# One memory map for the attention, index and sparse stages of a two-block transformer kernel, with the first loads of each stage issued in the stage ahead and the index tiles taken from most to fewest keys

## The chip, the cores and the metric

The kernel runs on one core of a Trainium2 chip. The metric is device time in microseconds (us), the median of several executions. Engines are called PE (TensorE), ACT (ScalarE), DVE (VectorE), POOL (GpSimd) and SP (SyncE, which here only issues DMAs).

## What is computed

A sequence of 2048 rows of width 1024 goes through two blocks. This case concerns the first, which joins a latent attention (MLA) and a sparse attention (DSA). Cut to what matters:

```python
h = rms_norm(x, norm_gain)
(c_q, c_kv, k_pe, gate_a, q_b, k_b, v_b, gate_b, q_i, k_i, w_i, m_a, m_b) = split(h @ w_in)
...
o_a = mla_attention(q_a, k_a, v_a) * silu(gate_a)            # 8 heads, causal, 96 wide
rel = relu(einsum('bqhd,bsd->bqhs', q_i, k_i))               # index: 8 heads, 32 wide
score = where(causal, einsum('bqhs,bqh->bqs', rel, w_i), -inf)
_, sel = top_k(score, 256)
o_b = attention over the keys in sel (8 heads, 2 kv heads) * silu(gate_b)
merged = sigmoid(m_a + b0) * (o_a @ w_branch_mla) + sigmoid(m_b + b1) * (o_b @ w_branch_dsa)
x = x + merged @ w_out
```

The second block (a window attention with sinks) follows and is not touched.

## The kernel before

The program is a row of stages, with a barrier of all engines between them (`sem.end_stage`, line 70 is where an engine waits at one): front (projections), MLA attention, index, sparse attention (DSA), merge, banded attention, final. Stages hand over through DRAM tensors (`scratch_...`). Products in high precision are three matmuls, hi and lo parts (`mm3`, lines 93 to 95).

**Front** (`stage_front`) computes, tile by tile of 128 rows, everything that the attentions read, and SP stores it to `scratch_qkT`, `scratch_va` and so on. Its loop counts slots n, twelve per row tile.

**Attention** (`stage_attention`, with a layer `Mla` or `Dsa`) works in 32 units. Of MLA, a unit is a head and a group of 512 rows (odd heads take the groups in reverse); of DSA a tile of 128 rows and one of two kv heads. For each unit PE makes scores, DVE adds the mask and takes the maximum (line 1042), ACT the exponential (1107), PE transposes (1012), ACT and DVE split into hi and lo (1115, 1072), PE multiplies with the values, POOL finishes the output. SP issues the loads of unit n + 4 (`layer.load`) and the stores of unit n - 1, in one queue.

**Index** (`stage_index`) does two things at once. One is the scores and the selection of 256 keys for row tiles 2 to 15 (tiles 0 and 1 have no more than 256 keys): step I is one head's product with up to 1024 keys (line 1409), then ACT's relu (1441) and DVE's weighted sum into `i_score` (1564, 1567); step M sets the bounds of a bisection (DVE 1574 to 1581, after POOL's mask); ten steps H halve it, each ACT's `Sign` with a count (1452) and then POOL's next threshold (1514, 1518); step T (DVE, 1587 to 1630) counts, and takes the rest with MAX8 and MATCH_REPLACE8; in it step R (PE, 1416) brings one number to one partition. POOL then stores the mask of the tile. The other is the gates: 24 chunks of 128 weight columns times 4 groups of 512 rows, that is 96 units of 8 steps G, each three matmuls of 128 x 512 (tile `i_p_g`, three banks), evacuated by ACT (1468, 1470) into two buffers and stored by SP. The weights come through one buffer `i_ws` and are split by ACT (step W, 1460) and DVE (1549).

`index_steps` writes the order of all these by hand: a tile's share of the G steps follows a cost, and its steps I and H are spread over that share. All engines walk the same list:

```python
marks += [((x + 0.5) / len(heads), 1, step) for x, step in enumerate(heads)]
marks += [((i + 0.5) / HALVINGS * 0.95, 0, ("H", before, i)) for i in range(HALVINGS)]
marks.append((AFTER_TOP / share, 2, ("R", after)))
```

So while PE and ACT do the I steps of tile t and the H steps of tile t - 1, DVE first has step T of tile t - 2. `i_relu` has three buffers, `i_p_s` two. Tiles go from 2 to 15, so the selection of the largest tile stands alone at the end. POOL loads the index queries of a tile in the middle of the halvings of the tile two before it (`load(t + 2)` after the sixth halving), four DMAs.

Every stage allocates its memory anew from the same base, so a stage's first loads are issued after the barrier: in MLA 5 DMAs per unit on SP for units 0 to 3, in index the weights, hT (the transposed input, 8 DMAs of 2 MB, for 4 groups) on SP and queries and keys on POOL, in DSA queries, mask, keys hi and lo and values in four groups on SP.

Of the kernel before, what the change touches and what calls it, by code (L numbers as in the profile page):

```python
# [22 lines left out]
P = 128  # L23
# [8 lines left out]
H = 8  # L32
# [107 lines left out]
def stage_front(nc, sem, ident, a, h_dram, qkT, qbT, kbT, qiT, kiT, va, vb, wi, bias):  # L140
# [18 lines left out]
    with ExitStack() as c:  # L159
# [95 lines left out]
        def _(sp):  # L255
# [558 lines left out]
class Attention:  # L814
# [26 lines left out]

    def sync_unit(self, sp, n): ...
# [54 lines left out]
def stage_attention(nc, sem, tag, ident, layer):  # L897
# [13 lines left out]
    with ExitStack() as c:  # L911
        sb = lambda n, s, d=F32: c.enter_context(nc.sbuf_tensor(f"{tag}_{n}", s, d))
        probs = sb("probs", [P, R, 4, layer.width])
# [21 lines left out]
        layer.setup(nc, sem, ident, c, dict(exped=exped, inverted=inverted, multiplied=multiplied, moved=moved,  # L935
# [23 lines left out]
        def _(pe):  # L959
# [37 lines left out]
            for step in steps:  # L997
# [8 lines left out]
                elif step[0] == "B":  # L1006
# [4 lines left out]
                    for s in range(s0, 4):  # L1011
                        last = nc.tensor.transpose(p_t[:, ring(n, place), s * P:(s + 1) * P],  # L1012
                                                   probs[:, n % R, s, j * P:(j + 1) * P], ident[:])
# [17 lines left out]
        def _(dve):  # L1031
            layer.dve_start(dve)
            i = 0
            for step in steps:
                if step[0] == "S":
                    _, n, s, ch, k0, w, last = step
                    if ch == 0:
# [5 lines left out]
                        out=probs[:, n % R, s, k0:k0 + w], in0=p_s[:, i % A, 0:w],  # L1043
# [53 lines left out]
        def _(act):  # L1097
            layer.act_start(act)
            for step in steps:
                if step[0] == "E":  # L1100
                    _, n, s = step
                    act.wait_ge(shifted, n + 1 if layer.batched else n_sub(n, s) + 1)
                    x = probs[:, n % R, s, 0:units[n]["keys"][s]]
# [38 lines left out]
class Mla(Attention):  # L1142

    scale = QK ** -0.5

    def __init__(self, qkT, va, oT, bias_job):
        self.qkT, self.va, self.oT, self.bias_job = qkT, va, oT, bias_job
# [4 lines left out]
                      for _, g in self.of]  # L1152

    def setup(self, nc, sem, ident, ctx, sems):
        sb = lambda n, s, d=F32: ctx.enter_context(nc.sbuf_tensor(f"mla_{n}", s, d))
        self.nc, self.sems = nc, sems
        self.q = [sb(f"q_{n}", [QK, 2, T], F32R) for n in ("hi", "lo")]
        self.k = [sb(f"k_{n}", [QK, 2, T], F32R) for n in ("hi", "lo")]
        self.v = sb("v", [P, 2, NT, P], F32R)
        self.none = sb("none", [P, GT])  # L1160
        self.causal = sb("causal", [P, GT])
        self.first_in, self.in_ = sem("mla_first_in", NG), sem("mla_in", 2)
# [23 lines left out]
    def load(self, sp, n):  # L1186
        h, g = n // NG, n % NG
# [10 lines left out]
        for half in range(2):  # L1198
            sp.dma_start(self.q[half][:, p, at].bitcast(F32), self.qkT[half, h, :, at]).then_inc(done, 16)
            sp.dma_start(self.k[half][:, p, at].bitcast(F32), self.qkT[half, H + h, :, at]).then_inc(done, 16)  # L1200
# [12 lines left out]
    def scores(self, out, n, s, k0, w):  # L1213
        p, t = n // NG % 2, self.of[n][1] * 4 + s
        q = [x[:, p, t * P:(t + 1) * P] for x in self.q]
        k = [x[:, p, k0:k0 + w] for x in self.k]
# [30 lines left out]
AFTER_TOP = 10  # L1247


def index_steps(tiles, chunks):  # L1250
# [5 lines left out]
    total = NG * len(gate_chunks()) * KD  # L1256
    tiles = list(tiles)
    keys = lambda t: P * (t + 1)
    cost = [0] + [8.5e-3 * (keys(t) + keys(t - 1)) + 7 for t in tiles[1:]] + [8.5e-3 * keys(tiles[-1]) + 20]
    steps, given = [("W", 0), ("W", 1)], 0  # L1260

    def give(count):
        nonlocal given
        for _ in range(min(count, total - given)):
            step, k = divmod(given, KD)
            steps.append(("G", step, k))
            given += 1
            if k == KD - 1 and step % NG == 0:
                n = step // NG + 1
                if 2 <= n < len(gate_chunks()):  # L1270
                    steps.append(("W", n))

    passed = 0
    for n, t in enumerate(tiles + [None]):
        before, after = tiles[n - 1] if n else None, tiles[n - 2] if n >= 2 else None
        passed += cost[n]
        share = int((total - AFTER_TOP) * passed / sum(cost) + 0.5) - given
        marks = []
        if t is not None:
            heads = [("I", t, h, k0, width) for h in range(H) for k0, width in chunks(t)]  # L1280
            marks += [((x + 0.5) / len(heads), 1, step) for x, step in enumerate(heads)]
        if before is not None:
            marks += [((i + 0.5) / HALVINGS * 0.95, 0, ("H", before, i)) for i in range(HALVINGS)]
        if after is not None:
            marks.append((AFTER_TOP / share, 2, ("R", after)))
# [1655 lines left out]
```

## Time and profile before

| | |
|---|---|
| median of 3 executions | 3502.67 us (3501.13 to 3503.57) |
| profiled execution, its own time | 3501.67 us |
| its span, first to last instruction | 3499.9 us |
| mean granted TensorE clock | 0.953 |
| MLA: first score to last matmul | 453.8 to 941.9 us |
| index: first DMA, last gate matmul | 948.7, 1649.1 us |
| DSA: first DMA, first score | 1668.9, 1682.6 us |

The profile is read in windows of time from the span's start. Busy time of PE counts matmuls that overlap in the pipeline, so the time of many is taken from the distance of their starts. PEclk is the granted clock as a share of 2.4 GHz; 0.5 is 1.2 GHz.

### The profile page before, as it was taken

Reading aid. Unit: us, or ns where it says so; the run is one execution under the profiler, and the core shown is the slowest. Engines: PE = TensorE matmul, PEld = TensorE weight load, DVE = VectorE, ACT = ScalarE, POOL = GpSimd, SP = SyncE. Lnnn points to the kernel's source line nnn. Section 1 sums busy time; section 2 is a strip of 40 time slices with the busy share of each in tenths; the row PEclk is TensorE's granted clock in tenths of the full one; section 3 lists DMA queues with packets and bytes.
Section 4 is the critical chain, followed back from the end, with each engine's and each line's share of the span. In section 5 each row is a group of like instructions: output and inputs, shape, how many; then the busy total and the mean of one; then the engine's idle time right before and its main releaser. Section 6 shows DMA issues by size and latency. Waiting matters only on the chain. (4 is left out here: it accounts for less than half of the span.)

```text
span 3499.9 us, 51538 instructions
## 1 busy us (share of the span) xinstructions
PE 3173.8 (91%) x17464; PEld 2674.8 (76%) x17464; DVE 2076.5 (59%) x5117; ACT 1820.6 (52%) x3608; POOL 789.4 (23%) x1091
## 2 busy tenths in 40 slices
PE   7999789999769889998599997899989999969998
PEld 5888668888657677776467776899878888869997
DVE  5776668888636555655599886544346666632112
ACT  5566457767536556574477775211146666632221
POOL 6444401111223212111111101111024444321110
PEclk9999989999979999999799998999999999969999
DMA  4666555343262222221621103444442222144332
GB/s 170 197 207 200 175 126 115 69 91 78 46 234 87 67 70 76 64 77 60 133 50 40 31 19 107 145 145 141 160 149 71 63 62 72 53 125 145 121 121 72
DMA packets 304565, 370.48 MB, mean 106 GB/s; under 512 B 22912, under 2 KB 248000, under 8 KB 300464
## 3 DMA queue, kind: packets, MB, share of 16 engines
q1 hardware_dynamic: 290480, 318.61, 31.7%
q0 software_dynamic: 13824, 48.58, 4.3%
q8 instruction: 140, 2.29, 0.3%
q14 instruction: 121, 0.99, 0.1%
HBM read 216.32 MB, written 150.80 MB: 105 GB/s over the span
## 5 line engine op out<-in xcount | busy, mean ns | idle before, releaser
L93 PE MATMUL i_p_g<-i_hT_lo,i_wh 128*128 128x512 f32 x768 | 310.5, 404 | 5.8 <-issue 5.5
L94 PE MATMUL i_p_g<-i_hT_hi,i_wl 128*128 128x512 f32 x768 | 306.3, 399 | 0.0
L95 PE MATMUL i_p_g<-i_hT_hi,i_wh 128*128 128x512 f32 x768 | 306.3, 399 | 0.0
L1567 DVE SCALAR_TENSOR_TENSOR i_score<-i_relu,i_w,i_score 128x1024 f32<-128x1024 f32 (+7 forms) x154 | 156.0, 1025 | 194.7 <-ACT i_relu L1441 192.5
L1452 ACT ACTIVATE i_above<-i_score,i_less 128x384 bf16<-128x384 f32 (+13 forms) x140 | 182.9, 1307 | 92.4 <-POOL i_less L1518 71.2
L1072 DVE TENSOR_TENSOR mla_tl<-mla_p_t,mla_th 128x512 fp32r<-128x512 f32 (+1 forms) x320 | 186.3, 606 | 45.6 <-ACT mla_th L1115 40.4
L1115 ACT ACTIVATE mla_th<-mla_p_t 128x512 fp32r<-128x512 f32 (+1 forms) x320 | 164.2, 530 | 87.1 <-PE mla_p_t L1012 84.1
L1441 ACT ACTIVATE i_relu<-i_p_s 128x1024 f32<-128x1024 f32 (+7 forms) x176 | 141.5, 810 | 126.0 <-DVE i_score L1564 83.9
L1042 DVE CUSTOM_DVE_ANT_0 dsa_probs<-dsa_p_s,dsa_mask 128x512 f32<-128x512 f32 (+3 forms) x320 | 184.6, 605 | 33.2 <-PE dsa_p_s L1696 32.0
L1072 DVE TENSOR_TENSOR dsa_tl<-dsa_p_t,dsa_th 128x512 fp32r<-128x512 f32 x272 | 179.8, 686 | 39.3 <-ACT dsa_th L1115 34.0
L1115 ACT ACTIVATE dsa_th<-dsa_p_t 128x512 fp32r<-128x512 f32 x272 | 155.0, 593 | 66.9 <-PE dsa_p_t L1012 66.0
L1695 PE MATMUL dsa_p_s<-dsa_k_hi,dsa_q 128*128 128x512 f32 (+3 forms) x320 | 132.8, 417 | 61.5 <-DMA dsa_v<-scratch_vb 33.5
L1107 ACT ACTIVATE dsa_probs<-dsa_probs,dsa_shift 128x128 f32<-128x128 f32 (+15 forms) x128 | 153.9, 1202 | 65.7 <-DVE dsa_shift L1064 65.0
L1012 PE MATMUL mla_p_t<-ident,mla_probs 128*128 128x128 f32 x1088 | 172.7, 274 | 10.8 <-DVE mla_tl L1072 9.4
L93 PEld LDWEIGHTS i_p_g<-i_hT_lo,i_wh 128*128 128x128 f32 x768 | 148.3, 193 | 39.4 <-issue 7.2
L93 PE MATMUL m_p_b<-m_ol,m_bh 128*128 128x256 f32 x512 | 149.2, 291 | 32.2 <-POOL m_ol L2562 28.2
L1107 ACT ACTIVATE mla_probs<-mla_probs,mla_shift 128x1280 f32<-128x1280 f32 (+15 forms) x128 | 153.6, 1201 | 44.8 <-DVE mla_shift L1064 43.3
L95 PEld LDWEIGHTS i_p_g<-i_hT_hi,i_wh 128*128 128x128 f32 x768 | 148.2, 193 | 34.3
L93 PE MATMUL b_p_p<-b_wl,b_xh 128*128 128x512 f32 (+1 forms) x384 | 161.7, 421 | 14.0 <-DVE b_wl L582 14.0
L1012 PE MATMUL dsa_p_t<-ident,dsa_probs 128*128 128x128 f32 x1088 | 167.4, 277 | 5.6 <-ACT dsa_probs L1107 2.7
L94 PEld LDWEIGHTS i_p_g<-i_hT_hi,i_wl 128*128 128x128 f32 x768 | 148.3, 193 | 30.1
L1012 PEld LDWEIGHTS dsa_p_t<-ident,dsa_probs 128*128 128x128 f32 x1088 | 132.3, 142 | 48.9 <-DVE dsa_tl L1072 19.5
(342 smaller groups left out, 9785.1 us busy)
## 6 DMA issues: line engine op xcount, KB each, us to landing
scratch_gates<-i_ob SPq DMA_DIRECT2D x96, 256.0 KB, 2.4
m_m<-scratch_gates SPq DMA_DIRECT2D x64, 256.0 KB, 4.2
f_hs<-scratch_h2T SPq DMA_DIRECT2D x16, 1024.0 KB, 10.2
scratch_qkT<-b_th SPq DMA_DIRECT2D x64, 192.0 KB, 2.6
scratch_qkT<-b_tl SPq DMA_DIRECT2D x64, 192.0 KB, 2.9
i_ws<-in_w_in SPq DMA_DIRECT2D x24, 512.0 KB, 4.6
b_xt<-in_x SPq DMA_DIRECT2D x16, 512.0 KB, 4.8
scratch_h<-b_xh POOLq DMA_DIRECT2D x16, 512.0 KB, 3.0
```

The costliest lines, as they stand in the source:

```text
L93: pe.matmul(out, l[0], r[1], start=start, stop=False)
L94: pe.matmul(out, l[1], r[0], start=False, stop=False)
L95: return pe.matmul(out, l[0], r[0], start=False, stop=stop)
L1012: last = nc.tensor.transpose(p_t[:, ring(n, place), s * P:(s + 1) * P], probs[:, n % R, s, j * P:(j + 1) * P], ident[:])
L1042: nc.vector.tensor_tensor_reduce(out=probs[:, n % R, s, k0:k0 + w], in0=p_s[:, i % A, 0:w], in1=layer.bias(n, s, k0, w), scale=1.0, scalar ...
L1072: nc.vector.tensor_tensor(tl[:, b % S, s0 * P:GT], p_t[:, ring(n, place), s0 * P:GT], th[:, b % S, s0 * P:GT].bitcast(F32), ALU.subtract). ...
L1107: nc.scalar.activation(x, x, ACT.Exp, bias=shift[:, n % R, s:s + 1], scale=layer.scale, accum_out=sums[:, n % R, s:s + 1]).then_inc(exped, 1)
L1115: nc.scalar.activation(th[:, b % S, s0 * P:GT], p_t[:, ring(n, place), s0 * P:GT], ACT.Copy).then_inc(hi_done, 1)
L1441: nc.scalar.activation(relu[:, n % 3, 0:width], p_s[:, n % 2, 0:width], ACT.Relu).then_inc(relued, 1)
L1452: nc.scalar.activation(above[:, 0:keys], score[:, t % 2, 0:keys], ACT.Sign, bias=less[:, t % 2:t % 2 + 1], accum_out=signs[:, i % 2:i % 2 ...
L1567: nc.vector.scalar_tensor_tensor(out=acc, in0=r, scalar=w[:, t, h:h + 1], in1=acc, op0=ALU.mult, op1=ALU.add).then_inc(summed, 1)
L1695: self.nc.tensor.matmul(out, q, self.k_hi[:, g, k0:k0 + w], start=True, stop=False)
```

## The change

- **Memory.** All of MLA's, index's and DSA's tensors get fixed places in one map (`at`, `kept`, `Space`); the first loads of a stage go to places that the stage ahead has done reading.
- **Front** (slot n = 193) issues the loads of MLA's unit 0 once all projections are done and the stores of the first four row tiles have landed.
- **MLA**: SP issues at unit 20 the index stage's first weights, two query tiles, the keys and small tensors (`load_first`), and at unit 28 hT of group 0 (2 x 2 MB, `load_h`).
- **Index**: hT of groups 1 to 3 is loaded at the start. Chunks 0 and 1 take each group in turn (`gate_order`), the others one after the other as before. Tiles go 15 to 2. I steps begin only after a part of the share that follows the length of the selection (`begin`), R's place follows the tile (`after_top`), and the cost counts the first tile. Before the last three gate units SP issues DSA's first queries, masks and keys hi (`load_early`), before the last two keys lo and values (`load_late`).
- **DSA**: keys and values are in two pieces instead of four groups, waited for before units 0 and 8.

```diff
+                if n == 12 * NT + 1:
+                    sp.wait_ge(projected, 3 * NT)
+                    for z in range(6 * 4 - S, 6 * 4):
+                        sp.wait_ge(t_stored[z % S], stored_until(z) + stores_of(z))
+                    sp.wait_ge(v_stored, 32 * 4)
+                    mla.load_unit(sp, 0)
...
     def sync_unit(self, sp, n):
         if n % NG == 2 and n // NG < self.bias_job.pieces:
             self.bias_job.store(sp, n // NG)
+        if n == NG * (H - 3):
+            self.index_in.load_first(sp)
+        if n == NG * (H - 1):
+            sp.wait_ge(self.sems["multiplied"], self.sems["n_b"][n])
+            self.index_in.load_h(sp, 0)
...
+def gate_order():
+    first = [(n, g) for g in range(NG) for n in range(PAIRED)]
+    return first + [(n, g) for n in range(PAIRED, len(gate_chunks())) for g in range(NG)]
...
-    cost = [0] + [8.5e-3 * (keys(t) + keys(t - 1)) + 7 for t in tiles[1:]] + [8.5e-3 * keys(tiles[-1]) + 20]
+    after_top = lambda t: 8 + int(5 * keys(t) / T)
+    selection = lambda t: 4 + 6.5e-3 * keys(t)
+    GATE = 0.68
+    cost = [8.5e-3 * keys(tiles[0])] + [8.5e-3 * (keys(t) + keys(b)) + 7 for b, t in zip(tiles, tiles[1:])] + [
+        8.5e-3 * keys(tiles[-1]) + 16]
...
-        share = int((total - AFTER_TOP) * passed / sum(cost) + 0.5) - given
+        share = int((total - 4) * passed / sum(cost) + 0.5) - given
...
-            marks += [((x + 0.5) / len(heads), 1, step) for x, step in enumerate(heads)]
+            begin = 0.6 * min(0.5, selection(after) / (share * GATE)) if after is not None else 0
+            marks += [(begin + (1 - begin) * (x + 0.5) / len(heads), 1, step) for x, step in enumerate(heads)]
...
-            marks.append((AFTER_TOP / share, 2, ("R", after)))
+            marks.append((after_top(after) / share, 2, ("R", after)))
...
+def index_tiles():
+    return list(range(NT - 1, TOPK // P - 1, -1))
...
+            for g in range(1, NG):
+                given.load_h(sp, g)
+                if g == 1:
+                    sp.wait_ge(w_split, 1)
+                    given.load_w(sp, 1)
+            for u, (n, g) in enumerate(order):
+                if u in load_at:
+                    sp.wait_ge(w_split, load_at[u])
+                    given.load_w(sp, load_at[u])
+                if u == len(order) - 3:
+                    sp.wait_ge(filled, u)
+                    sp.wait_ge(stored, 32)
+                    after.load_early(sp)
+                elif u == len(order) - 2:
+                    sp.wait_ge(filled, u)
+                    after.load_late(sp)
...
+    pieces = (slice(0, GT), slice(GT, T))
+    def load_early(self, sp):
+        self.load_queries(sp, 0)
+        for x in range(2):
+            self.load_keys(sp, x, self.k_hi, 0)
+        self.load_queries(sp, 1)
+    def load_late(self, sp):
+        for x, at in enumerate(self.pieces):
+            self.load_keys(sp, x, self.k_lo, 1)
+            sp.dma_start(self.v[:, at.start // P:at.stop // P].bitcast(F32),
+                         self.vb[at].rearrange("(j p) (g e) -> p j g e", p=P, g=KV)).then_inc(self.kv_in[x], 16)
```

Three places show how the instructions move. The first is SP's queue at the start of the index stage (`i_ws` weights, `i_hT_hi`, `i_hT_lo` the transposed input by groups, `i_ob` finished gates). Before, from the branch that opens the stage's loads:

```order
L1374 DMA i_ws<-in_w_in 128x8x128
L1377 DMA i_bias_m<-in_b_merge 128x16x1
L1382 DMA i_hT_hi<-scratch_h 128x4096
L1382 DMA i_hT_lo<-scratch_h 128x4096
L1374 DMA i_ws<-in_w_in 128x8x128
L1382 DMA i_hT_hi<-scratch_h 128x4096
L1382 DMA i_hT_lo<-scratch_h 128x4096
```

and now:

```order
L1464 UNCONDITIONAL_BRANCH
L1373 DMA i_hT_hi<-scratch_h 128x4096
L1373 DMA i_hT_lo<-scratch_h 128x4096
L1378 DMA i_ws<-in_w_in 128x8x128
L1373 DMA i_hT_hi<-scratch_h 128x4096
L1373 DMA i_hT_lo<-scratch_h 128x4096
L1373 DMA i_hT_hi<-scratch_h 128x4096
L1373 DMA i_hT_lo<-scratch_h 128x4096
L1484 DMA scratch_gates<-i_ob 128x512 x2
```

The first weights and group 0 are gone from the stage; the second weights stand behind the 4 MB of group 1, and the first gate stores behind all groups.

The second is ACT's order where a tile's scores have just ended (`i_relu` relu of an I step, `i_above` a halving, `i_ob` a gate evacuation, `i_wh` a weight split). Before, from tile 12's last relu-and-evacuation on, with the first relu of tile 13 ahead of the first halving of tile 12 (1664 keys):

```order
L1470 ACTIVATE i_ob<-i_p_g,i_bias_m 128x512
L1441 ACTIVATE i_relu<-i_p_s 128x1024
L1452 ACTIVATE i_above,i_signs<-i_score,i_less 128x1664
L1470 ACTIVATE i_ob<-i_p_g,i_bias_m 128x512
L1441 ACTIVATE i_relu<-i_p_s 128x768
L1452 ACTIVATE i_above,i_signs<-i_score,i_less 128x1664
L1441 ACTIVATE i_relu<-i_p_s 128x1024
L1470 ACTIVATE i_ob<-i_p_g,i_bias_m 128x512
```

and now, at the first halvings of tile 11 (1536 keys), with tile 10's relus behind:

```order
L1534 ACTIVATE i_relu<-i_p_s 128x512
L1544 ACTIVATE i_above,i_signs<-i_score,i_less 128x1536
L1562 ACTIVATE i_ob<-i_p_g,i_bias_m 128x512
L1552 ACTIVATE i_wh<-i_ws 128x1024
L1544 ACTIVATE i_above,i_signs<-i_score,i_less 128x1536
L1562 ACTIVATE i_ob<-i_p_g,i_bias_m 128x512
L1534 ACTIVATE i_relu<-i_p_s 128x1024
```

Two evacuations and two halvings now stand between the last relu of one tile and the first of the next.

The third is SP's queue at the end of the index stage, now (before, the eight last gate stores are one run and all `dsa_` loads come behind the barrier):

```order
L1770 DMA dsa_q<-scratch_qbT 64x8x128 x2
L1773 DMA dsa_mask<-scratch_mask 128x128
L1758 DMA dsa_k_hi<-scratch_kbT 64x2x512 x2
L1758 DMA dsa_k_hi<-scratch_kbT 64x2x1536 x2
L1770 DMA dsa_q<-scratch_qbT 64x8x128 x2
L1773 DMA dsa_mask<-scratch_mask 128x256
L1484 DMA scratch_gates<-i_ob 128x512
L1758 DMA dsa_k_lo<-scratch_kbT 64x2x512 x2
L1751 DMA dsa_v<-scratch_vb 128x4x256
L1758 DMA dsa_k_lo<-scratch_kbT 64x2x1536 x2
L1751 DMA dsa_v<-scratch_vb 128x12x256
L1484 DMA scratch_gates<-i_ob 128x512 x2
```

Sixteen DMAs, 7 MB, stand ahead of the last two gate stores.

## Rows read from the trace of the kernel before

**Rows 1.** The page's first part: busy time, share of the span, instructions.

```profile
PE 3173.8 (91%) x17464; PEld 2674.8 (76%) x17464; DVE 2076.5 (59%) x5117; ACT 1820.6 (52%) x3608; POOL 789.4 (23%) x1091
```

**Rows 2.** Windows of time, index stage's dense part: us, busy PE PEld DVE ACT POOL, PEclk, DMA, GB/s.

```profile
986.80:1649.10 662.30, 612.84 (x2615) 495.93 (x2614) 365.37 (x661) 395.59 (x570) 149.60 (x371) 0.97 0.27 86
```

**Rows 3.** Timeline, start of MLA, SP and PE: start, us, engine, line, [idle before].

```profile
446.03 0.32 SPq L1199 DMA_DIRECT2D mla_q_hi<-scratch_qkT  x1
...
453.77 0.47 PE L93 MATMUL mla_p_s<-mla_k_lo,mla_q_hi 96*128 96x128 f32 x1 [20.36 <-DMA mla_v<-scratch_va]
...
457.83 0.79 PE L93 MATMUL mla_p_s<-mla_k_lo,mla_q_hi 96*128 96x512 f32 x1 [0.17 <-DMA mla_v<-scratch_va]
```

**Rows 4.** Timeline, start of the index stage: SP, PE, SP, ACT.

```profile
948.68 0.40 SPq L1374 DMA_DIRECT2D i_ws<-in_w_in  x1
...
975.26 1.01 PE L1409 MATMUL i_p_s<-i_k,i_q 128*128 128x384 f32 x2 [33.36 <-DMA i_k<-scratch_kiT]
...
976.50 0.38 SPq L1374 DMA_DIRECT2D i_ws<-in_w_in  x1
...
981.59 1.06 ACT L1460 ACTIVATE i_wh<-i_ws 128x1024 fp32r<-128x1024 f32 x1 [24.57 <-DMA i_ws<-in_w_in]
```

**Rows 5.** Timeline of PE in a stretch of gates alone, first and last of 39.

```profile
1639.96 0.39 PE L93 MATMUL i_p_g<-i_hT_lo,i_wh 128*128 128x512 f32 x1
...
1648.58 0.39 PE L95 MATMUL i_p_g<-i_hT_hi,i_wh 128*128 128x512 f32 x1
```

**Rows 6.** Waits, index stage: who for whom, us in total, times, longest.

```profile
PE i_p_s L1409 <- ACT i_relu L1441: 48.2, 14, 6.8
```

**Rows 7.** Timeline, one selection (tile 12): DVE, DVE, ACT, PE, PE.

```profile
1468.28 0.16 DVE L1587 TENSOR_TENSOR i_mid<-i_widths,i_less 128x1 f32<-128x1 f32 x1
...
1485.80 1.03 DVE L1630 TENSOR_SCALAR i_bias<-i_score 128x1664 bf16<-128x1664 f32 x1 [0.23 <-issue]
...
1487.78 0.92 ACT L1441 ACTIVATE i_relu<-i_p_s 128x896 f32<-128x896 f32 x1 [11.42 <-DVE i_score L1564]
...
1488.75 0.68 PE L1409 MATMUL i_p_s<-i_k,i_q 128*128 128x512 f32 x2 [3.40 <-ACT i_relu L1441]
...
1490.06 0.63 PE L95 MATMUL i_p_g<-i_hT_hi,i_wh 128*128 128x512 f32 x1
```

**Rows 8.** Timeline of ACT, halvings of tile 3 (512 keys).

```profile
1027.32 0.72 ACT L1452 ACTIVATE i_above<-i_score,i_less 128x512 bf16<-128x512 f32 x1 [0.25 <-POOL i_less L1518]
1028.98 0.72 ACT L1452 ACTIVATE i_above<-i_score,i_less 128x512 bf16<-128x512 f32 x1 [0.26 <-POOL i_less L1518]
...
1044.63 0.72 ACT L1452 ACTIVATE i_above<-i_score,i_less 128x512 bf16<-128x512 f32 x1 [6.24 <-POOL i_less L1518]
```

**Rows 9.** Timeline: DVE's selection of tile 2 from R on; of tile 15; SP.

```profile
1026.79 0.28 DVE L1605 TENSOR_REDUCE i_rounds<-i_p_l 1x1 f32<-1x128 f32 x1 [0.81 <-PE i_p_l L1416]
...
1031.31 0.36 DVE L1630 TENSOR_SCALAR i_bias<-i_score 128x384 bf16<-128x384 f32 x1 [0.27 <-issue]
...
1662.82 1.23 DVE L1630 TENSOR_SCALAR i_bias<-i_score 128x2048 bf16<-128x2048 f32 x1 [0.23 <-issue]
...
1668.86 1.33 SPq L1663 DMA_DIRECT2D dsa_q<-scratch_qbT  x2
```

**Rows 10.** Timeline, start of DSA: PE's first score, ACT's wait at tile 2.

```profile
1682.55 0.44 PE L1695 MATMUL dsa_p_s<-dsa_k_hi,dsa_q 128*128 128x128 f32 x1 [33.48 <-DMA dsa_v<-scratch_vb]
...
1710.27 0.62 ACT L1107 ACTIVATE dsa_probs<-dsa_probs,dsa_shift 128x384 f32<-128x384 f32 x1 [8.34 <-DVE dsa_shift L1064]
```

**Rows 11.** Windows of time: while hT loads, and while DSA's inputs load.

```profile
985.00:990.00 5.00, 4.93 (x12) 3.46 (x12) 3.94 (x7) 1.96 (x4) 1.47 (x4) 0.50 1.00 426
1684.00:1686.00 2.00, 2.00 (x11) 2.00 (x11) 1.83 (x15) 2.00 (x9) 0.00 (x0) 0.50 1.08 241
```

**Rows 12.** DMA issues: one output store behind DSA's loads (1665 to 1705 us); all.

```profile
scratch_obT<-dsa_ot SPq DMA_DIRECT2D x1, 128.0 KB, 6.2
scratch_obT<-dsa_ot SPq DMA_DIRECT2D x32, 128.0 KB, 2.5
```

More of the change, by code:

```diff
@@ L1264, in give @@
         for _ in range(min(count, total - given)):
-            step, k = divmod(given, KD)
-            steps.append(("G", step, k))
+            u, k = divmod(given, KD)
+            steps.append(("G", u, k))
             given += 1
[L1268 to L1271, printed above, removed]
+            chunk, g = order[u]
+            if k == KD - 1:
+                if (chunk, g) == (0, NG - 1):
+                    steps.append(("W", 2))
+                elif (chunk, g) == (2, 1):
+                    steps.append(("W", 3))
+                elif g == 0 and 3 <= chunk < len(gate_chunks()) - 1:
+                    steps.append(("W", chunk + 1))
     passed = 0
@@ L1310, in stage_index @@
+def stage_index(nc, sem, ident, given, space, mask, gates, after):
     with ExitStack() as c:
-        sb = lambda n, s, d=F32: c.enter_context(nc.sbuf_tensor(f"i_{n}", s, d))
-        hT = [sb(f"hT_{n}", [P, NT, KD, P], F32R) for n in ("hi", "lo")]
-        ws = sb("ws", [P, KD, P])
+        sb = lambda n, s, d=F32: space(f"i_{n}", s, d)
+        hT, q, k, w, bias_m, ws = given.hT, given.q, given.k, given.w, given.bias_m, given.ws
+        k_in, q_in, h_in, bias_in, w_loaded = given.k_in, given.q_in, given.h_in, given.bias_in, given.w_loaded
@@ L1402, in _ @@
                     _, t, h, k0, width = step
+                    x = place[t]
                     if h == 0 and k0 == 0:
-                        pe.wait_ge(q_in[t % 2], 64 * ((t - tiles[0]) // 2 + 1))
+                        pe.wait_ge((q_in if x < 2 else q_later)[x % 2], 64 * max(1, x // 2))
                     if n >= 2:
                         pe.wait_ge(relued, n - 1)
-                    for x in range(0, width, GT):
-                        y = min(GT, width - x)
-                        last = nc.tensor.matmul(p_s[:, n % 2, x:x + y], q[:, t % 2, h],
-                                                k[:, k0 + x:k0 + x + y], start=True, stop=True)
+                    for y in range(0, width, GT):
+                        z = min(GT, width - y)
+                        last = nc.tensor.matmul(p_s[:, n % 2, y:y + z], q[:, x % 2, h],
+                                                k[:, k0 + y:k0 + y + z], start=True, stop=True)
                     last.then_inc(scored, 1)
@@ L1418, in _ @@
                     _, u, b = step
-                    chunk, g = divmod(u, NG)
+                    chunk, g = order[u]
                     if b == 0:
@@ L1554, in _ @@
                 t = step[1]
-                keys = P * (t + 1)
-                s = score[:, t % 2, 0:keys]
+                x, keys = place[t], P * (t + 1)
+                s = score[:, x % 2, 0:keys]
                 if step[0] == "I":
@@ L1637, with __init__ @@
     scale = HD ** -0.5
-    def __init__(self, qbT, kbT, vb, mask, oT):
-        self.qbT, self.kbT, self.vb, self.mask, self.oT = qbT, kbT, vb, mask, oT
+    tag = "dsa"
+    def __init__(self, nc, qbT, kbT, vb, mask, oT, early, late):
+        self.nc, self.qbT, self.kbT, self.vb, self.mask, self.oT = nc, qbT, kbT, vb, mask, oT
+        self.k_hi = early("dsa_k_hi", [P, KV, T], F32R)
+        self.q = early("dsa_q", [P, 2, H, P], F32R)
+        self.m = early("dsa_mask", [P, 2, T], BF16)
+        self.k_lo = late("dsa_k_lo", [P, KV, T], F32R)
+        self.v = late("dsa_v", [P, NT, KV, P], F32R)
+        self.q_in, self.m_in, self.kv_in = ([nc.alloc_semaphore(name=f"dsa_{n}{x}") for x in range(count)]
+                                            for n, count in (("q_in", 2), ("m_in", 2), ("kv_in", 2)))
@@ L1655, in load, with load_keys @@
+    def load_keys(self, sp, x, dst, half):
+        at = self.pieces[x]
+        src = self.kbT[half].rearrange("(g d) t -> d g t", d=HD)[:, :, at]
+        for rows in (slice(0, HD), slice(HD, P)):
+            sp.dma_start(dst[rows, :, at].bitcast(F32), src).then_inc(self.kv_in[x], 16)
     def load(self, sp, n):
         t, g = n // KV, n % KV
-        if g:
+        if t < 2 or g:
             return
-        if t >= 2:
-            sp.wait_ge(self.sems["moved"], self.sems["n_s"][KV * (t - 1)])
```

288 lines of the change are left out of this document (151 added, 137 removed).

## The prediction

> **What bounds the kernel now.** I read the page first, then the windows around the three stage borders that the change touches, then the timelines there, last the waits of the index stage. PE is busy 91% of the span [rows 1], so time comes back only where PE idles or runs at a low clock. It does so at the borders. At the start of MLA it waits from the last stage to 453.77, 7.7 us after SP's first load at 446.03, and once more until 457.83 for the second unit's loads [rows 3]. In the index stage the first DMA is issued at 948.68, the first score starts at 975.26, and then everything waits again: the second weights are issued only at 976.50, since DVE waits for the keys ahead of its first split, and ACT, in order, passes them at 981.59 [rows 4]; the gates begin at 986.8. DSA's first score starts at 1682.55, 13.7 us after its first DMA at 1668.86 [rows 9, 10].
>
> Inside the index stage, 986.8 to 1649.1, PE is busy 612.8 of 662.3 us, at a mean clock of 0.97 [rows 2]. Its work there is less. A gate matmul takes 0.227 us (38 steps in 8.62 us) [rows 5]; 768 steps of three are 522.3 us. The index products have 8 heads x 17,024 keys (128 x (3 + ... + 16)), that is 266 matmuls of 512 columns, 60.3 us at 0.227, of which 1.4 lie before 986.8. With 2 us for the R steps the sum is 583.2. The stage thus loses 79.1 us: 49.5 idle, about 20 to 1.2 GHz (a mean of 0.97 is that level for 6% of the time, 40 us at half speed), and 10 of small things. The idle time is a pattern that comes once per tile: PE waits 48.2 us, in 14 pieces, for a relu [rows 6]. For tile 12 DVE is in step T from 1468.28 to 1486.83, 18.6 us; the three relu buffers are full, ACT stands 11.42 us in order behind the next relu, PE stops 3.40 us, and afterwards a matmul takes 0.63 us instead of 0.39, at 1.2 GHz [rows 7].
>
> **The change, part by part.**
>
> MLA's start. Unit 0's five loads are issued in front about when SP has nothing to do, 2.5 us of issue, hidden. Unit 0's scores can start at once, but unit 1's loads now go first after the barrier and land as unit 0's did, 7.7 us after 446.03. So unit 1 starts at 453.8 instead of 457.83: 4.0 us gained. Ends: 0 if DVE and ACT set the pace anyway, 7.5 if all of the first wait counts.
>
> MLA's loads for the index stage. About 22 more DMAs on SP, 7 MB. Units 20 to 23 and 28 to 31 last some 60 us per head (488 us for eight), the transfers take under 30. The output stores queue behind them, as one did for 6.2 instead of 2.5 us [rows 12], and have two units of slack. Nothing; at worst 4 us.
>
> The index stage's opening. Before, 38.1 us from first DMA to gates hold 1.4 us of work: 36.7 lost. Now ACT and DVE split the first weights at once (1.1 and 1.2 us), which lets SP issue the second weights at about +3. They stand behind the 4.2 MB of group 1. At 426 GB/s [rows 11] that takes 10 us, with the weights' 0.5 MB and their landing +13; at 241 GB/s it would be +20. ACT splits them, and being in order only then does its first relu, at +14. PE does about 3 us of its steps until then and stands. Some 23 us of the first tile's 27 us are left, and PE begins at 1.2 GHz, 4 us more: the first tile (29 G, 32 index matmuls) ends at +41. Lost: 14. Ends 10 and 22. Gain 22.7. Groups 2 and 3 land by +23 and +33; PE wants group 2 at G step 32, after that. The first gate stores also wait until +33, and ACT needs the first of them free at G step 24, at +36.
>
> The body. The same steps in another order; the question is what of the 79.1 us stays. After T of a 1536-key tile has begun, the new order gives PE 13 G steps before the next I step, then an I every three. DVE needs 4.5 us from a tile's last I to T and 18 us for it, 33 G steps; ACT sticks at the fourth relu, step 22 to 25, and PE would only stop at the sixth I, step 29 with 2 us of index products in between: about even. So the stops of 3 to 6 us become 1 to 2 us. Large tiles: 9 x 1.5 = 14 us. The low clock goes with them, except for some 10 us of time lost in small gaps. Small tiles come last now and are bound by the halvings: 1.66 us per step at 512 keys, and one pause of about 8 us (a wait of 6.24) while POOL issues the next mask and queries [rows 8]. Ten halvings plus 4.5 us to the next bounds make 33, 31, 29.5 and, without queries to load, 23.5 us for tiles 6, 5, 4, 3, where PE has 30.6, 26.8, 24.2 and 20.4 us of steps: 15 us over, of which the last tile, with 28 us of steps for a chain of 20, returns a few: 12. Kept: 14 + 10 + 12 = 36. Gain 43. Ends: kept 15 (the small tiles alone) and 79 (nothing gained).
>
> First the rows on the clock: in tile 12 it fell right behind the stop and came back with steady matmuls [rows 7], and I gave the 20 us back with the stops. The Trainium skill, "TensorE: Matmul & The Clock Gate", section "What's actually happening", says that the throttled clock is the default and activity releases it; by it those 20 us return, by a low clock that comes regardless the time would be 20 us higher, 3425.
>
> The end. Now 19.8 us pass from PE's last gate to 1668.86. DVE's part, 1649.1 to 1664.05, shrinks: for 384 keys it takes 4.9 us from R on (1026.79 to 1031.67) [rows 9]. With the same 4.8 us to the next stage that is 10.1. But 7 MB of loads are issued from 16.3 us (three units of 5.44) before PE's end, and the last gate stores queue behind. At 241 GB/s they take 29 us, to +13; with the store's landing the next stage starts at +13.5. Gain 6.3. Ends +10.1 and +20.
>
> The Trainium skill, "DMA: Bandwidth & Descriptors", section "Issuing engines are not separate DMA queues", says that DMAs of all issuing engines interleave on the same 16 engines. By it the last mask store, though on POOL's queue, shares the delay; were it free of it and the gates too, the sum would be 3 us lower. No row shows the two kinds there.
>
> DSA's start. Keys and values land before the barrier, so PE's first score comes 0.3 us after it: 13.4 gained. The wait of 8.34 us at tile 2 for queries and mask that stood behind the keys [rows 10] goes as well, 8.2. Ends 13.4 and 24. Gain 21.6.
>
> Sum: 4.0 + 22.7 + 43 + 6.3 + 21.6 = 97.6 us, from the profiled execution's own 3501.67 to 3404. The median shown is 1.0 above that execution: **3405**.
>
> **The rivals.**
>
> A. The order gives nothing: the stops only move, since ACT, 60% busy in the stage and more in the part of a tile where the I steps now crowd, becomes late instead. For it: at three G steps per I (2.4 us) relu, halving and evacuation fill some 2.1 us of ACT. Against: the wait in rows 7 is DVE's, and ACT's own work did not stop PE. Time: 3405 + 43 = 3448.
>
> B. The queue bites at both ends: second weights at 241 GB/s (+8 us) and the next stage at +20 (+6.5). 3405 + 15 = 3420.
>
> C. Slower: the halving chain sits in ACT's order, and each POOL pause (6.24 us in rows 8) now holds relus that are packed densely. Place: the middle of every tile. It decides from the point where PE loses the 79 us of before plus the 55 gained elsewhere, 134 us in 14 tiles, 9.6 us per tile. At 10.5 us per tile the time is 3515. Against: each pause is 8 us once per tile and PE has two score buffers and three gate banks, over 10 us of steps, to pass it.
>
> D. The early loads don't take effect (a wait in SP's queue keeps them until the stage's end) and the order gives nothing: 3500. The waits named in the diff are all on work finished by then.
>
> **How the numbers follow.** Forecast 0.72, A 0.17, B 0.08, C 0.02, D 0.01. The predicted time is the forecast's. Its own bounds (3386 with 18 us less kept and lost, 3436 with the body at 60 and the ends late) and A at 3448 set the range 3386 to 3450. A measurement of this kernel can tell 0.2% (7 us) from no change: faster by more 0.96, the same 0.02, slower 0.02.
>
> **What would show it.** Right: MLA's second unit about 7.7 us after the first DMA; in index the second weight split at +14 and the first tile's end at +41; PE's waits for relu down from 48 us to under 20, and a clock of 0.98 or more in the body; PE's last gate 632 us after the stage's first DMA; DSA's first score within 1 us of its barrier. Wrong: relu waits as large as before with another cause (A), a split at +20 or gate stores landing last by far (B), PE waiting on `i_above` evacuations for 10 us in each tile (C).

## The result and the profile after

The changed kernel takes **3425.34 us** (median of 4 executions, 3419.67 to 3426.81) against 3501.9 us for the kernel before beside it: a ratio of 0.9784, 95% interval 0.977 to 0.9798. The forecast was 3405 in a range of 3386 to 3450. The direction held, and so did the mechanisms at MLA's start, in the opening and in the body; 20 us of the 98 forecast are missing, about half in the body, where a matmul took longer than priced, and half at the stage's end. The profiled execution's span is 3422.5 us, 77.4 less than before, and splits like this in the two traces ("last gate" is its end here):

| stretch | before | after | change | forecast |
|---|---|---|---|---|
| start to the index stage's first DMA | 948.7 | 943.3 | -5.4 | -4.0 |
| from there to PE's last gate | 700.3 | 645.9 | -54.4 | -65.7 |
| last gate to DSA's first score | 33.6 | 24.5 | -9.0 | -19.7 |
| DSA's first score to the end | 1817.3 | 1808.8 | -8.6 | -8.2 |

(The last forecast is the wait at tile 2; the third is 6.3 + 13.4. The last row varies by some 5 us between traces of the same instructions: 1805.7 to 1810.7 us in the eight kernels below whose DSA stage and loads are the changed kernel's, and 1812.5 in the kernel before with 576 bytes moved; so part of its agreement is luck.) The page's first line after, and windows of the index stage as in [rows 2], whole, opening and body:

```profile
PE 3171.4 (93%) x17464; PEld 2665.5 (78%) x17464; DVE 2079.6 (61%) x5117; ACT 1820.8 (53%) x3608; POOL 775.1 (23%) x1078
```

```profile
945.87:1589.20 643.33, 616.03 (x2622) 491.40 (x2622) 377.49 (x675) 399.95 (x576) 145.77 (x371) 0.98 0.31 97
943.27:990.10 46.83, 37.53 (x140) 29.76 (x141) 22.11 (x29) 21.56 (x23) 2.32 (x7) 0.84 0.79 316
990.10:1589.20 599.10, 578.50 (x2484) 461.67 (x2482) 356.99 (x658) 379.45 (x554) 144.62 (x368) 0.99 0.27 80
```

PE idles 20.6 us in the body, where it idled 49.5 in the dense part before, and the granted clock there is 0.99 for 0.97. In the body it fell to 1.2 GHz three times, each time right behind a stop of PE (2.5, 2.9 and 3.8 us); before, nine times, in or right behind stops of 1.9 to 6.6 us. The borders, in the timeline of the changed kernel (MLA's unit 1; the index stage's first DMA, first gate, second weight split, the stop behind it, the last index product of tile 15; 39 gate matmuls in a row, first and last; ACT's last evacuation; DSA's first score):

```profile
453.54 0.79 PE L93 MATMUL mla_p_s<-mla_k_lo,mla_q_hi 96*128 96x512 f32 x1 [3.46 <-DMA mla_v<-scratch_va]
...
943.27 0.33 SPq L1373 DMA_DIRECT2D i_hT_hi<-scratch_h  x1
945.87 0.77 PE L93 MATMUL i_p_g<-i_hT_lo,i_wh 128*128 128x512 f32 x1 [9.29 <-DVE i_wl L1632]
957.66 1.06 ACT L1552 ACTIVATE i_wh<-i_ws 128x1024 fp32r<-128x1024 f32 x1 [13.25 <-DMA i_ws<-in_w_in]
959.68 1.22 PE L1502 MATMUL i_p_s<-i_k,i_q 128*128 128x512 f32 x2 [6.70 <-ACT i_relu L1534]
985.18 0.62 PE L1502 MATMUL i_p_s<-i_k,i_q 128*128 128x512 f32 x2
...
1579.94 0.40 PE L93 MATMUL i_p_g<-i_hT_lo,i_wh 128*128 128x512 f32 x1
...
1588.80 0.40 PE L95 MATMUL i_p_g<-i_hT_hi,i_wh 128*128 128x512 f32 x1
...
1594.63 0.69 ACT L1562 ACTIVATE i_ob<-i_p_g,i_bias_m 128x512 f32<-128x512 f32 x1 [9.71 <-DMA scratch_gates<-i_ob]
...
1613.74 0.44 PE L1789 MATMUL dsa_p_s<-dsa_k_hi,dsa_q 128*128 128x128 f32 x1 [24.43 <-PEq L70]
```

Two things in it were not forecast. The 38 steps from 1579.94 to 1588.80 take 8.86 us, 0.2332 us each, where [rows 5] had 0.2268 for the same stretch of gates alone. Over the whole stage the mean of all distances between 0.20 and 0.26 us from one matmul's start to the next is 0.2330 for 0.2291 before. And ACT's last evacuation waits 9.71 us for a buffer whose gate store stands in SP's queue behind DSA's loads. Windows from SP's first DSA load until the last gate store has landed (1612.5), the DMAs of 1573 to 1616 us in all, and the last mask store (KB, us to landing) show the transfers without a pause until then, at 204, 244 and 218 GB/s:

```profile
1573.60:1590.00 16.40, 15.71 (x68) 12.30 (x66) 2.33 (x11) 4.23 (x12) 3.69 (x12) 1.00 0.96 204
1590.00:1608.00 18.00, 0.00 (x0) 0.00 (x0) 2.51 (x13) 0.69 (x1) 0.89 (x2) 0.58 1.08 244
1608.00:1612.60 4.60, 0.00 (x0) 0.00 (x0) 0.00 (x0) 0.00 (x0) 0.00 (x0) 0.50 0.63 218
```

```profile
DMA packets 6306, 8.74 MB, mean 203 GB/s; under 512 B 480, under 2 KB 4720, under 8 KB 6304
...
scratch_mask<-i_bias POOLq DMA_DIRECT2D x1, 96.0 KB, 9.0
```

The waits that answer to [rows 6] fell from 48.2 to 25.7 us. Of the 48.2, 6.8 lie ahead of 986.8, and of the 25.7, 6.7 lie in the opening, so the body's went from 41.4 to 19.0:

```profile
PE i_p_s L1502 <- ACT i_relu L1534: 25.7, 14, 6.7
```

### The profile page after: what moved, and what is told of

The parts are those of the page before. It is cut to its first block and busy times, and to the rows that moved or that the text cites. A ratio compares the mean times of both kernels' runs of the same rounds, so it can differ in the third digit from the quotient of the medians.

```text
span 3422.5 us, 51529 instructions
## 1 busy us (share of the span) xinstructions
PE 3171.4 (93%) x17464; PEld 2665.5 (78%) x17464; DVE 2079.6 (61%) x5117; ACT 1820.8 (53%) x3608; POOL 775.1 (23%) x1078
## 5 line engine op out<-in xcount | busy, mean ns | idle before, releaser
L1544 ACT ACTIVATE i_above<-i_score,i_less 128x2048 bf16<-128x2048 f32 (+13 forms) x140 | 183.2, 1308 | 106.6 <-POOL i_less L1601 69.6
L1534 ACT ACTIVATE i_relu<-i_p_s 128x1024 f32<-128x1024 f32 (+7 forms) x176 | 141.6, 813 | 77.4 <-DVE i_score L1647 38.8
```

Of the source, the lines that this page charges most:

```text
L1534: nc.scalar.activation(relu[:, n % 3, 0:width], p_s[:, n % 2, 0:width], ACT.Relu).then_inc(relued, 1)
L1544: nc.scalar.activation(above[:, 0:keys], score[:, x % 2, 0:keys], ACT.Sign, bias=less[:, x % 2:x % 2 + 1], accum_out=signs[:, i % 2:i % 2 ...
```

## The experiments

Three questions were open: what in the new order removes the stops (and whether the order does it at all), where the pace of 0.233 comes from, and what each border still costs. Twelve kernels ran. The first columns are distances of starts in each trace (MLA's last matmul to PE's last gate; last gate to DSA's first score), then PE's waits for relus, the pace of the last 38 gate steps (from the trace's times in ns; rows rounded to 0.01 us give 0.2332 and 0.2266 to 0.2268), and the ratio to the kernel before on the same chip with its interval.

| kernel | to last gate | to DSA | relu waits | pace | ratio |
|---|---|---|---|---|---|
| before | 707.0 | 34.0 | 48.2 | 0.2267 | |
| changed | 652.5 | 24.9 | 25.7 | 0.2333 | 0.9784 [0.977, 0.9798] |
| e1_old_order | 692.2 | 25.7 | 55.0 | 0.2333 | 0.99 [0.9882, 0.9919] |
| e2_w1_first | 654.5 | 24.2 | 26.8 | 0.2333 | 0.9796 [0.9777, 0.9815] |
| e3_small_first | 652.1 | 16.5 | 24.8 | 0.2333 | 0.9754 [0.9733, 0.9775] |
| e4_no_early | 651.4 | 34.8 | 23.5 | 0.2333 | 0.9809 [0.9792, 0.9827] |
| e5_old_marks | 708.2 | 23.4 | 65.5 | 0.2333 | 0.9945 [0.9928, 0.9962] |
| e6_opening | 643.2 | 24.7 | 18.6 | 0.2333 | 0.9749 [0.9733, 0.9765] |
| e7_weights_place | 646.5 | 26.9 | 31.6 | 0.2267 | 0.9762 [0.9743, 0.9781] |
| e8_base_place | 650.2 | 24.2 | 24.5 | 0.2333 | 0.9777 [0.9761, 0.9793] |
| e9_all | 639.5 | 16.3 | 25.0 | 0.2267 | 0.9706 [0.9688, 0.9725] |
| e10_all_paired_end | 643.6 | 11.6 | 24.2 | 0.2267 | 0.971 [0.969, 0.9729] |
| e11_top_old | 647.1 | 25.1 | 23.4 | 0.2333 | 0.9759 [0.9736, 0.9781] |
| e12_before_moved | 714.9 | 34.2 | 47.6 | 0.2333 | 1.0008 [0.9997, 1.002] |

One caution on the times: MLA's last matmul falls between 936.3 and 941.4 us in the changed kernel and in the eleven variants of it, whose instructions are the same up to there. The intervals of single edits of 5 to 8 us therefore overlap; the distances decide. These come from one trace of each kernel: in the four kernels that share the changed kernel's order, opening and placement (changed, e3, e4, e8) the first is 650.2 to 652.5, and in the seven that share its end (changed, e2, e5 to e8, e11) the second is 23.4 to 26.9.

**The order of the tiles** (the old list in the new memory map):

```diff
-    return list(range(NT - 1, TOPK // P - 1, -1))
+    return list(range(TOPK // P, NT))
-            begin = 0.6 * min(0.5, selection(after) / (share * GATE)) if after is not None else 0
+            begin = 0
-    after_top = lambda t: 8 + int(5 * keys(t) / T)
+    after_top = lambda t: 10
```

and the old cost (0 for the first tile, 20 and not 16 for the end, 10 steps kept back).

> The changed kernel with the index tiles from 2 to 15 again and the old rules of the list (cost, I steps from the start of a share, R at 10 steps); memory map and early loads stay. Theory 1 (the order took stops and low clock out of the body): the stops of 3 to 7 us per tile are back, PE waits about 45 us for relus, and the stage from its first gate on loses 35 to 45 us more: about 3460. Rival (the order gave nothing, the body gained by the loads alone): 3425 to 3430. On the pace: if the gate matmuls' 0.233 us (0.2295 before) comes with the memory map, it stays 0.233 here; if it comes with the order (a PE that is not interrupted), it falls back to 0.2295.

Measured: 3467.72, 42 us above the changed kernel. PE's first gate comes 17 us later after the stage's first DMA, since tile 2's few products leave PE nothing to do until the second weights are there (a stop of 14.8 us); so that part of the opening's gain, too, needs the largest tile first. From first to last gate it is 665.5 for 642.9 us: 22.6 us for the body, less than the 35 to 45 expected, with waits for relus of 40.2 for 25.7 behind the first gate. The new list as a whole does gain, and the pace stays 0.2333: it comes with the map.

**The late begin and R's place taken back**, tiles from 15 to 2:

> Tiles from 15 to 2 as changed, but the I steps are spread over the whole share and R stands at 10 steps, as before. Theory 1 (the late begin is what shortens the stops behind a selection): PE's waits for relus in the body go from 19 us back to about 40, the low clock with them, and the time is 15 to 25 us more than the changed kernel's, about 3445. Rival (the order of the tiles alone took the stops, with the old marks they stay short): within 5 us of the changed kernel.

Measured: 3479.2, 54 us above the changed kernel and 11 above the old order (698.6 us from first to last gate for 642.9 and 665.5). Neither guess was near: descending tiles with the old marks are the worst of the three lists. The selection of tile 12 in that run (DVE's T, its end, ACT's next relu, PE's next index product):

```profile
1240.10 0.16 DVE L1670 TENSOR_TENSOR i_mid<-i_widths,i_less 128x1 f32<-128x1 f32 x1
...
1259.09 1.03 DVE L1713 TENSOR_SCALAR i_bias<-i_score 128x1664 bf16<-128x1664 f32 x1 [0.35 <-issue]
...
1261.07 0.49 ACT L1534 ACTIVATE i_relu<-i_p_s 128x384 f32<-128x384 f32 x1 [13.85 <-DVE i_score L1647]
...
1261.61 0.69 PE L1502 MATMUL i_p_s<-i_k,i_q 128*128 128x384 f32 x1 [6.84 <-ACT i_relu L1534]
```

and the same selection in the changed kernel:

```profile
1221.64 0.16 DVE L1670 TENSOR_TENSOR i_mid<-i_widths,i_less 128x1 f32<-128x1 f32 x1
...
1239.89 1.03 DVE L1713 TENSOR_SCALAR i_bias<-i_score 128x1664 bf16<-128x1664 f32 x1 [0.35 <-issue]
...
1242.81 0.49 ACT L1534 ACTIVATE i_relu<-i_p_s 128x384 f32<-128x384 f32 x1 [6.74 <-DVE i_score L1647]
...
1243.36 0.44 PE L1502 MATMUL i_p_s<-i_k,i_q 128*128 128x384 f32 x1 [2.49 <-ACT i_relu L1534]
```

T is about as long in both (20.0 and 19.3 us). Where the next tile's I steps begin late, the three relu buffers fill later: ACT stands 6.74 us and not 13.85 (11.42 in [rows 7]), PE 2.49 and not 6.84. So descending tiles gain nothing without the late begin (the next run shows that R's place is not what counts). Why they are worse than the old list then is not shown; it may be that the next products meet the longer selection of a larger tile. Nor was the late begin tried with tiles from 2 to 15, so what the order of the tiles adds to it in the body is open.

**R's place alone taken back** (`after_top` = 10, late begin kept):

> The changed kernel with R at 10 gate steps for every tile, the late begin of the I steps kept. With both old marks the time was 3479. Theory: the late begin alone is what counts, and the place of R is worth 3 us or less: 3420 to 3430. Rival (R's place holds T back by as much as the begin gives): 3440 or more.

Measured: 3419.92, at the low edge. The new rule for R gains nothing; to the last gate it was 5.4 us shorter without it. This kernel and e5_old_marks differ in the late begin alone, so 61 us to the last gate hang on that line.

**The opening.** The second weights ahead of all of hT:

```diff
-            for g in range(1, NG):
-                given.load_h(sp, g)
-                if g == 1:
-                    sp.wait_ge(w_split, 1)
-                    given.load_w(sp, 1)
+            sp.wait_ge(w_split, 1)
+            given.load_w(sp, 1)
+            for g in range(1, NG):
+                given.load_h(sp, g)
```

> The second weights are issued ahead of group 1 of hT in place of behind it. Theory 1: their split comes at +5 in place of +14.4 after the stage's first DMA, the stop of 6.7 us and the low clock behind it go, group 1 lands 3 us later, at +14, when PE has just come to want it: 7 to 9 us less, about 3417. Rival: the 4 MB of group 1, issued 3 us later, become what PE waits for at gate step 16, and the gain is 3 us or less.

Measured: 3430.73, no gain. DVE's split did come 4.8 us after SP's first DMA and the first stop went, but at +37 and +38.5 this stood in ACT's and PE's timeline:

```profile
985.63 0.60 ACT L1559 ACTIVATE i_ob<-i_p_g 128x512 f32<-128x512 f32 x1 [12.79 <-DMA scratch_gates<-i_ob]
...
987.20 1.22 PE L1501 MATMUL i_p_s<-i_k,i_q 128*128 128x512 f32 x2 [10.30 <-ACT i_relu L1533]
```

The third evacuation needs a buffer whose store is behind 12.6 MB of hT. PE had come there earlier than before, and only waited longer. Neither theory had named this stop, though the prediction's own text had the store at +33. So the next kernel also moved `load_h` of group 3 behind the first two gate stores:

> Second weights first, then hT groups 1 and 2, and group 3 only behind the first two gate stores. Theory 1 (in the run with the weights first, the stop of 10.3 us came from gate stores that queued behind 12 MB of hT; with group 3 behind them both stops go): from the stage's first gate to its last 633 to 636 us in place of 643, some 8 us less than the changed kernel. Rival (DVE and ACT cannot take the I steps of tile 15 at PE's full pace, so the stop only moves): 640 us or more, no gain.

Measured: 3413.44; first gate to last 633.6 us. Of the two stops 0.8 us are left, though ACT still waits for the first gate store:

```profile
973.95 0.60 ACT L1561 ACTIVATE i_ob<-i_p_g 128x512 f32<-128x512 f32 x1 [3.27 <-DMA scratch_gates<-i_ob]
...
975.52 0.73 PE L1503 MATMUL i_p_s<-i_k,i_q 128*128 128x512 f32 x2 [0.78 <-ACT i_relu L1535]
```

The opening's 9 us were a matter of one queue's order.

**The pace.** First the place of the split weights (two small tensors go to the top of the memory):

```diff
+            end = (end - 576) // 32 * 32
-        self.w = sb("w", [P, NT, H])
-        self.bias_m = sb("bias_m", [P, 16])
+        self.w = top("i_w", [P, NT, H], F32)
+        self.bias_m = top("i_bias_m", [P, 16], F32)
```

> Only the places of two small tensors are changed, so that the split weights lie 151,552 bytes behind hT hi (4096 over a multiple of 16,384, as before the change) and not 152,128. Theory P1 (the place of the stationary against the moving tensor sets the pace): the gate matmuls' 0.2333 us falls to 0.227 to 0.2295 and the stage is 10 to 15 us shorter. Theory P2 (the place of hT itself does) and P3 (neither place does): 0.2333 stays, no gain.

then the whole map up by 512 bytes:

> The whole map is moved up by 512 bytes: hT hi at 19,136, which is the place before the change (17,088) plus 2048. Theory P2 (the place of hT itself sets the pace): the gate matmuls go from 0.2333 us to 0.227 to 0.2295, and the stage is 10 to 15 us shorter. Theories P1 and P3: 0.2333 stays.

then the other way round, in the kernel before:

```diff
         ws = sb("ws", [P, KD, P])
+        bias_m = sb("bias_m", [P, 16])
+        w = sb("w", [P, NT, H])
         wh = sb("wh", [P, 2, KD, P], F32R)
```

> The kernel BEFORE the change, with its two small tensors of the index stage (512 and 64 bytes) between hT and the split weights, which then lie 135,744 bytes behind hT hi and not 135,168 (33 x 4096). Nothing else differs. Theory P1: the gate matmuls in the stretch of gates alone go from 0.2269 to 0.2333 us, and the time rises by 3 to 10 us. If the place is not the cause: 0.2269 stays.

The first and last of the 39 matmuls ahead of the stage's end, with the weights moved, and below in the kernel before with the 576 bytes between:

```profile
1577.47 0.39 PE L93 MATMUL i_p_g<-i_hT_lo,i_wh 128*128 128x512 f32 x1
...
1586.08 0.39 PE L95 MATMUL i_p_g<-i_hT_hi,i_wh 128*128 128x512 f32 x1
```

```profile
1648.65 0.39 PE L93 MATMUL i_p_g<-i_hT_lo,i_wh 128*128 128x512 f32 x1
...
1657.51 0.39 PE L95 MATMUL i_p_g<-i_hT_hi,i_wh 128*128 128x512 f32 x1
```

Measured: 3418.84, 3422.46, and 3505.53 against 3502.55 for the kernel before beside it. 8.61 us (0.2266 each) and 8.86 (0.2332): the 576 bytes change the pace in both directions, and the move of everything by 512 bytes does nothing. The gain was smaller than expected: with 2570 matmuls at 0.2278 for 0.2330 some 13 us, of which PE's waits for relus take back 5.9 (31.6 for 25.7); to the last gate 6.0 us are left. In the kernel before the slower pace costs 8 us of the stage and 0.08% of the time, which its interval does not tell from nothing. In both runs the split weights, hi and lo, and the gates' output buffer moved by 576 bytes, and others beside them, so that it is the weights is an inference from the stretch in which PE reads nothing else but hT. Whether their distance from hT counts (P1) or their own place is not settled either. By the places on record the weights start at 152,256 and 170,176 in the fast kernels, 192 over a multiple of 512, and at 152,832, 170,752 and 171,264 in the slow ones, 256 over one. A move of 512 bytes keeps both that remainder and the distance, so the run cannot tell them apart; a move of everything by 448 bytes would have, which keeps the distance and brings the weights to 192 over a multiple. Other remainders were not tried.

**The end.** The second pieces of keys and values, 4.5 MB, behind the last gate stores (`load_rest` after the loop of gate units):

> At the end of the index stage the second pieces of DSA's keys and values (4.5 MB of 7) are issued behind the last gate stores in place of ahead of them. Theory 1 (the last two gate stores queue behind the loads and hold the barrier): PE's last gate to DSA's first score falls from 24.7 us to 13 or 14, about 3414; unit 8 of DSA does not wait. Rival (the 16 DMA engines are shared, so the mask store and the gate stores are as slow whatever stands ahead of them): 21 us or more, 3422 or above.

Measured: 3416.71; last gate to first score 16.5 for 24.9 us. Theory 1 to a good part (13 or 14 expected), and the rival for the rest: the gates no longer wait, but the mask store on POOL's queue took as long as ever beside SP's loads:

```profile
scratch_mask<-i_bias POOLq DMA_DIRECT2D x1, 96.0 KB, 9.1
```

All of DSA's loads behind the barrier:

> DSA's first loads are issued behind the barrier, all else as changed. Theory 1: PE's last gate to the stage's end falls from 24.4 us to about 10 (DVE's last selection, the mask store, the barrier), but DSA's first score comes 13 us or more after its first DMA, as before, and a wait of up to 8 us at tile 2 is back: 3425 to 3433, so that the early loads as placed are worth under 8 us of the 28 that were forecast. Rival (the early loads gain what was forecast, 6.3 at the end and 21.6 at the start): 3445 or more.

Measured: 3434.21, so the early loads as placed are worth 9 us, of 28 forecast. PE's end to the first DMA was 8.8 us, as expected; but the first score came 25.6 us after it and not 13 or more, since both pieces of keys hi now stand ahead of lo and values. In return no wait of 8 us comes at tile 2: from first DMA to the end it is 1832.6 us for 1831.0 before, so the new order of DSA's loads gains nothing by itself. The estimate of its total was 1 us low.

**All together**, and then with chunks 22 and 23 taking the groups in turn at the end as 0 and 1 do at the start, and all of DSA's loads issued ahead of the last two gate stores, from six gate units before the end:

> The edits of three runs together: second weights first and hT group 3 behind two gate stores, the large pieces of DSA's keys and values behind the last gate stores, and the split weights at a multiple of 4096 from hT. If they are independent: 12 + 8 + 6 us less than the changed kernel, about 3400; if the faster matmuls only wait more (PE's waits grew by 7 us in the run with the weights moved), 3403 to 3407.

> As the run before in the opening and in the place of the weights; at the end chunks 22 and 23 take the groups in turn, so that DSA's loads start six gate units before the end and are spread over them. Theory: the queue is nearly empty when the last selection ends, the mask store lands in 4 to 5 us and not 9, and PE's last gate to DSA's first score is 10 to 12 us (16 with the large pieces behind): 4 to 6 us less than the run before, about 3396. Rival (a gate store behind a piece of 1.5 MB holds ACT and PE inside the last units, or the third split stalls PE): no gain, and PE stops in the last 35 us.

Measured: 3401.27 (ratio 0.9706, 0.9688 to 0.9725), the best kernel of this study with the next, and 3400.81, the same within the intervals. The first is 24 us less than the changed kernel, near the 26 of edits that add up. In the second the border did what was expected, 11.6 us, with the mask store down to 2.0 us:

```profile
scratch_mask<-i_bias POOLq DMA_DIRECT2D x1, 96.0 KB, 2.0
```

and the rival took it back, in one stop of PE for the split of chunk 23, which DVE does only after the selection of tile 4 (ACT's part, DVE's selection and split, PE):

```profile
1531.15 1.05 ACT L1563 ACTIVATE i_wh<-i_ws 128x1024 fp32r<-128x1024 f32 x1
...
1538.62 0.49 DVE L1724 TENSOR_SCALAR i_bias<-i_score 128x640 bf16<-128x640 f32 x1 [0.22 <-issue]
1539.03 1.22 DVE L1643 TENSOR_TENSOR i_wl<-i_ws,i_wh 128x1024 fp32r<-128x1024 f32 x1
...
1540.30 0.79 PE L93 MATMUL i_p_g<-i_hT_lo,i_wh 128*128 128x512 f32 x1 [6.53 <-DVE i_wl L1643]
```

## Why the prediction was right, and where it was 20 us off

**MLA's start: right.** Unit 1 starts at 453.54 (453.8 forecast). That the stretch gave 5.4 us and not the forecast 4.0 says little, since MLA's end varies by 5 us between runs of the same code.

**The opening: right.** The second split stands at +14.4 (14 forecast), PE ends tile 15's products at 985.8, +42.5 (41 forecast). The loss is 42.5 less 119 matmuls of 0.2268, 15.5 us for 14. That the queue cost 9 us of it is shown by the run in which of both stops 0.8 us were left.

**The body: right mechanism, work under-priced.** PE's last gate ends 645.9 us after the stage's first DMA; the text had 632, itself 3 less than the sum's terms give. Of the forecast 36 us kept, 26 were stops, 14 for the large tiles and 12 for tiles 6 to 3; PE idles 20.6 us, of it 13.5 up to the end of tile 7's selection at 1459 and 6.8 behind it. So the large tiles came out as priced and the small ones at about half. The clock came back with the stops: it is 0.99 in the body. The step that failed is the price of the work, "a gate matmul takes 0.227 us", taken from a row of the kernel before and held for the kernel after. 2451 matmuls at 0.2330 are 15.2 us more. The forecast had 10 us for all small things, the low clock with it; here these are 10.0, and with the pace 25.2: 45.8 kept for 36. The price was low for the kernel before as well, 0.2291 over its stage, which is 6 us of what the text booked there as "small things". I had read the diff's memory map for what it lets start early, and never asked where it puts the operands of the dominant instruction. [rows 6] was read a little wide, too: of 49.5 us idle 41.4 and not 48.2 were waits for relus, and one stop of 5.5 us at 1013.20 was not.

Rival A (stops only move) fell: the old list costs 22.6 us from first to last gate. I wrote of the new order as one thing, but what the text argues from, 13 G steps before the next I step, is the late begin, and the runs show that the gain hangs on it: tiles from most to fewest keys without it are 11 us slower than the old list.

**The end and DSA's start: 10.7 us short.** The score did come with the barrier (PE's last wait, in the row above, is for it) and the wait at tile 2 went (-8.6 for -8.2). The failing step is "At 241 GB/s they take 29 us, to +13; with the store's landing the next stage starts at +13.5". The start was nearly right (15.6 us before PE's end for 16.3, 0.7 lost). But 8.74 MB pass and not 7: the last four gate stores (1.0 MB), two mask stores (0.2) and what my 7 had rounded off (0.4), 7.2 us at 241 GB/s. And the rate was 204 GB/s while PE still worked and 244 only behind its end; over the 38.9 us until the last gate store landed (23.3 us behind PE's end) it was about 225, which is 2.7 us more. DSA's first score came 1.2 us behind that landing. So of rival B the half at the stage's end came true, while the weights' half did not.

**The two pages.** In the index stage's body the clock fell to 1.2 GHz only in or right behind stops, nine times before and three times after, and came back with steady matmuls. This agrees with the Trainium skill, "TensorE: Matmul & The Clock Gate", section "What's actually happening", by which the throttled clock is the default and activity releases it. That the mask store on POOL's own queue took 9.0 us beside SP's loads and 2.0 without them agrees with the Trainium skill, "DMA: Bandwidth & Descriptors", section "Issuing engines are not separate DMA queues".

## What to carry to other kernels

A load that is moved ahead of a border also moves ahead of the stores that hold the border: price every byte in that queue, the stores among them, up to the barrier, and issue first only what the next stage's first step needs. A stop between engines that is taken away at one place shows what is late next (here, in the opening, a buffer that waits for its store), so change the queue's order for both at once. And a new memory map can change the duration of the instruction that it was not made for: compare the start distances of the dominant instruction, in a stretch where it runs alone, before anything else.

## What was not expected of the hardware

The place in memory of the weights, which each float32 matmul of 128x512 loads for itself, changed its pace: 0.2267 us from start to start where they lie a multiple of 4096 bytes behind hT hi (33 and 37 times), 0.2333 where they lie 576 bytes over one, in the traces of four and ten kernels, and it changed with 576 bytes in the kernel before as in the kernel after. Whether the distance from the moving operand or the weights' own place counts is open. The Trainium skill, "TensorE: Matmul & The Clock Gate", section "Step-by-step: what each phase is for", says that PE has two independent read ports, so that loading weights takes no bandwidth from the running matmul. By it the distance between the two should not matter; if the distance is the cause, these runs differ from the page, and the measurement decides. If it is the weights' own place, they don't. The 3% in the stretch of gates alone are measured either way.
